# The output projection taken in thirds of its k tiles over six PSUM banks, with four expert weight pieces requested during it

## The reference

```python
def _mixer(h, ..., w_out):
    z = einsum('btd,de->bte', h, w_in) + b_in            # one input projection, 11 groups of 512
    y_r = ...    # RG-LRU group, 512 columns
    y_h = ...    # HGRN2 group, 512 columns
    y_m = sigmoid(m_o) * head_layer_norm(mlstm)          # mLSTM group, 4 heads of 128 columns
    y = concatenate([y_r, y_h, y_m], -1)                 # 1536 columns
    return einsum('bte,ed->btd', y, w_out)               # the output projection

def _layer(...):
    y = _mixer(x * (1 + sc1) + sh1, ...)
    x = layer_norm(ALPHA * x + g1 * y) * ln1_g + ln1_b
    f = _moe(x * (1 + sc2) + sh2, ...)                   # router softmax over 16 experts, best group of 4, top 2
    return layer_norm(ALPHA * x + g2 * f) * ln2_g + ln2_b

def _moe(h, ...):
    act = silu(h @ w_gate[e]) * (h @ w_up[e]) * combine  # per expert: 1024x512, 1024x512
    return act @ w_down[e]                               # 512x1024
```

## Time and profile before

| | |
|---|---|
| median of 3 runs | 750.0 us (749.65 to 751.92) |
| the profiled execution, its time | 752.23 us |
| the profiled execution, its span | 750.5 us |
| TensorE busy | 684.4 us (91%), weight loads 550.6 us |
| VectorE busy | 575.3 us (77%) |
| ScalarE busy | 433.5 us (58%) |
| GpSimd busy | 57.8 us (8%) |
| DMA | 220.06 MB, mean 293 GB/s |

### The profile page before, as it was taken

One profiled execution on the slowest core, in us unless ns is written; L12 is line 12 of the kernel. 1 busy time (PEld: TensorE's weight loads), 2 busy tenths in 40 slices (PEclk: granted clock), 3 DMA queues, 4 the chain that ended last, 5 costly groups with the idle time before them and its releaser, 6 DMA issues.

```text
span 750.5 us, 12527 instructions
## 1 busy us (share of the span) xinstructions
PE 684.4 (91%) x4818; PEld 550.6 (73%) x4818; DVE 575.3 (77%) x838; ACT 433.5 (58%) x605; POOL 57.8 (8%) x88
## 2 busy tenths in 40 slices
PE   4599989999899979999995989999999999999881
PEld 2487988898689879964454968888888888888640
DVE  2659797798993456773777878989999999999765
ACT  1647857363133445750124458888888888888721
POOL 2060000000011000132000300000000000000210
PEclk9699999999999999999996999999999999999996
DMA  9997596546758697969008999999999999999442
GB/s 334 374 244 289 203 347 230 210 155 201 279 200 280 232 396 274 334 48 385 25 0 326 411 385 396 400 398 400 400 399 400 400 399 399 400 399 400 152 144 84
DMA packets 91507, 220.06 MB, mean 293 GB/s; under 512 B 3335, under 2 KB 3631, under 8 KB 91455
## 3 DMA queue, kind: packets, MB, share of 16 engines
q1 hardware_dynamic: 85200, 200.29, 71.7%
q0 software_dynamic: 5840, 18.94, 8.4%
q10 hardware_dynamic: 415, 0.14, 0.1%
HBM read 179.99 MB, written 39.36 MB: 292 GB/s over the span
## 4 chain that ended last, share of the span: by engine, by line
PE 66%; DVE 15%; DMA 9%; ACT 4%; issue 3%; SPq 1%; POOL 1%; DVEq 0%; ACTq 0%; POOLq 0%
PE ps L1169 63%; DMA ring<-in_w_in 3%; DMA extra<-slot_rows 2%; DMA arena<-in_pos 2%; PE ps L1566 2%; DVE w_lo L1729 2%; DMA slot_rows<-arena,small 2%; DVE arena L1884 1%; DVE arena L1883 1%; DVE arena L1829 1%; PE ps L1585 1%; POOL slot_rows L749 1%; DMA ring<-in_w_gate 1%; ACT w_hi L826 1%; SPq L550 1%
## 5 line engine op out<-in xcount | busy, mean ns | idle before, releaser
L2181 DVE TENSOR_TENSOR w_lo<-arena,w_hi 128x1024 fp32r<-128x1024 f32 x96 | 114.6, 1220 | 13.8 <-ACT w_hi L1054 12.8
L2181 DVE TENSOR_TENSOR w_lo<-ring,w_hi 128x1024 fp32r<-128x1024 f32 x96 | 114.9, 1220 | 10.9 <-ACT w_hi L1054 9.8
L1054 ACT ACTIVATE w_hi<-ring 128x1024 fp32r<-128x1024 f32 x96 | 100.6, 1062 | 23.3 <-PE ps L1169 19.3
L1054 ACT ACTIVATE w_hi<-arena 128x1024 fp32r<-128x1024 f32 x96 | 100.8, 1063 | 19.6 <-PE ps L1169 13.7
L1169 PE MATMUL ps<-h_hi,w_lo 128*128 128x384 f32 x288 | 102.0, 354 | 9.4 <-DVE w_lo L1729 6.0
L1169 PE MATMUL ps<-w_hi,slot_tokens_lo 128*128 128x512 f32 x256 | 103.0, 402 | 0.8 <-DVE w_lo L2181 0.8
L1169 PE MATMUL ps<-w_hi,slot_tokens_hi 128*128 128x512 f32 x256 | 100.2, 391 | 0.0
L1169 PE MATMUL ps<-w_lo,slot_tokens_hi 128*128 128x512 f32 x256 | 99.8, 390 | 0.0
L1169 PE MATMUL ps<-h_lo,w_hi 128*128 128x384 f32 x288 | 97.5, 338 | 0.0
L1169 PE MATMUL ps<-h_hi,w_hi 128*128 128x384 f32 x288 | 97.4, 338 | 0.0
L1729 DVE TENSOR_TENSOR w_lo<-ring,w_hi 128x1024 fp32r<-128x1024 f32 x44 | 53.6, 1224 | 23.3 <-ACT w_hi L826 22.2
(11 more groups left out here) (361 smaller groups left out, 1102.7 us busy)
## 6 DMA issues: line engine op xcount, KB each, us to landing
slot_rows<-arena SPq DMA_DIRECT2D x12, 2048.0 KB, 18.3
ring<-in_w_in SPq DMA_DIRECT2D x11, 2048.0 KB, 10.0
ring<-in_w_ada SPq DMA_DIRECT2D x10, 2048.0 KB, 9.0
ring<-in_w_gate SPq DMA_DIRECT2D x8, 2048.0 KB, 18.2
ring<-in_w_up SPq DMA_DIRECT2D x8, 2048.0 KB, 18.5
ring<-in_w_down SPq DMA_DIRECT2D x8, 2048.0 KB
arena<-in_w_gate SPq DMA_DIRECT2D x8, 2048.0 KB, 18.3
arena<-in_w_down SPq DMA_DIRECT2D x8, 2048.0 KB, 14.9
```

The source lines that it names most:

```text
L1054: act.activation(w_hi[:, at_ % 4, :], raw[:, q * QUARTER:(q + 1) * QUARTER], ACT.Copy).then_inc(S["hi_ready"], 1)
L2181: tt(w_lo[:, at_ % 4, :], raw[:, q * QUARTER:(q + 1) * QUARTER], w_hi[:, at_ % 4, :].bitcast(F32), ALU.subtract).then_inc(S["lo_dve"], 1)
```

## The change

The projection is done in three sweeps. `project_all(part)` runs over all six banks with the 4 k tiles of one third of w_out: first YR, then YH. Then come the last 4 k tiles (YM) bank by bank, where the router's work is interleaved as it was. The transposes of the last mLSTM head now stand behind the first sweep, and go to bank 7 instead of bank 2. Bank waits that the order needs are added (t_taken for bank 1, cfin_sb for bank 2, h_done for bank 5).

When a sweep is over, its ring slot is free (semaphore wout_used), and SyncE requests expert weights into it: the gate of expert 2 after the first sweep, the up piece of expert 0 after the second; the down piece of expert 0 is requested at y_ready as before. The gate of expert 0 goes to a new place, `first_gate`, which is the area of `w_lo`, as soon as the last unit of the mixer's weights has been used. VectorE writes the low parts of that gate over it, quarter by quarter. `residual(1)` moves from the loop over row tiles to `last_rows`. Three one-shot semaphores become one (consts_made). The number of matmuls and the bytes moved are the same.

```diff
@@ SyncE @@
                 sp.wait_ge(S["h2_ready"], 1)
                 expert_piece(bass.ds(1, 1), 0, 1)
                 expert_piece(bass.ds(1, 1), 2, 1)
-                sp.wait_ge(S["lo_dve"], MIX_DVE + 4)
-                expert_piece(bass.ds(2, 1), 0, 0)
...
+            sp.wait_ge(S[USED[-1][0]], USED[-1][1])
+            src = a["w_gate"][0][0:1].rearrange("a (k p) n -> p (a k) n", p=P)
+            sp.dma_start(first_gate.rearrange("p (k n) -> p k n", k=KD), src).then_inc(S["gate0_in"], 16)
+            sp.wait_ge(S["wout_used"], 1)
+            expert_piece(bass.ds(2, 1), 0, 0)
+            sp.wait_ge(S["wout_used"], 2)
+            expert_piece(bass.ds(0, 1), 1, 0)
             sp.wait_ge(S["y_ready"], 2 * NT)
-            first_experts(0)
+            expert_piece(bass.ds(0, 1), 2, 0)
@@ TensorE @@
-            for m in WOUT:
-                full(m)
-            project(0, 0, range(0, 4))
+            def project_all(part):
+
+                full(WOUT[part])
+                for i in range(NT):
+                    for half in range(2):
+                        if part == 0 and (i, half) == (0, 1):
+                            pe.wait_ge(S["t_taken"], H - 1)
+                        if part == 0 and (i, half) == (1, 0):
+                            pe.wait_ge(S["cfin_sb"], 16)
+                        if part == 0 and (i, half) == (2, 1):
+                            pe.wait_ge(S["h_done"], 7)
+                        last = project(i, half, range(4 * part, 4 * part + 4))
+                last.then_inc(S["wout_used"], 1)
+
+            project_all(0)
+            normed_T(H - 1, ps[:, 7, :])
             pe.wait_ge(S["yh_full"], 1)
-            project(0, 0, range(4, 8))
-            pe.wait_ge(S["cfin_sb"], 16)
-            normed_T(H - 1, ps[:, 2, :])
-            project(0, 1, range(0, 8))
+            project_all(1)
...
             pe.wait_ge(S["ym_done"], 2)
+            full(WOUT[2])
             for i in range(NT):
-                project(i, 0, range(8 if i == 0 else 0, 12)).then_inc(S["y_ready"], 1)
+                project(i, 0, range(8, 12)).then_inc(S["y_ready"], 1)
...
-                project(i, 1, range(8 if i == 0 else 0, 12)).then_inc(S["y_ready"], 1)
+                project(i, 1, range(8, 12)).then_inc(S["y_ready"], 1)
@@ VectorE @@
                 mixed_half(i, 0)
                 router_logits(i - 1)
                 selection(i - 1)
-                residual(i - 1)
+                if i == 1:
+                    residual(0)
                 mixed_half(i, 1)
...
             def last_rows():
 
-                residual(NT - 1)
+                for i in (1, 2):
+                    residual(i)
```

More of the change, by code:

```diff
@@ L494, in build @@
                     for j, x in enumerate(("hi", "lo"))]
+        first_gate = place("first_gate", o_conv + PIECE, PIECE)
         PICK = place("picked_rows", o_conv + 2 * PIECE, 6 * D).rearrange("p (c i d) -> p c i d", c=2, i=NT)
@@ L847, in _ @@
                     act.wait_ge(S["z_ready"], Z_READY[job])
-                    act.wait_ge(S["silu_zeroed"], 1)
+                    act.wait_ge(S["consts_made"], 1)
                     act.activation(silu_w[:, 0:16].rearrange("p (k s) -> p s k", s=2), bank[:, 0:16].rearrange("p (s k) -> p s k", s=2),
@@ L1059, in landed @@
                     return ring2_full[j], 16 * pair + 16
-                return ring_full[(FIRST_EXPERT + j) % NSLOT], 16 * pair + 16 * ((FIRST_EXPERT + j) // NSLOT + 1)
+                before = (FIRST_EXPERT + j) // NSLOT
+                return ring_full[(FIRST_EXPERT + j) % NSLOT], 16 * pair + 16 * (before if j == 0 else before + 1)
             def silu(n):
@@ L1108, in expert_pass @@
                 p0 = base // 2
-                gate = expert_slot(0, 0)
+                gate = expert_slot(0, 0) if base else first_gate
                 for q in range(4):
-                    hi(base, q, gate, q, landed(0, p0, 0) if q == 0 else None)
+                    hi(base, q, gate, q, (landed(0, p0, 0) if base else (S["gate0_in"], 16)) if q == 0 else None)
                 tokens_hi(base, 0)
@@ L1309, in _ @@
                     pe.wait_ge(S[sem], value)
-                    pe.wait_ge(S["sel_ready"], 1)
+                    pe.wait_ge(S["consts_made"], 3)
                     b = job[1] // 2 % 2 if job[1] < 4 else job[1] % 2
@@ L1352, in _ @@
                     if (q, k0) == (0, 0):
-                        pe.wait_ge(S["banks_cleared"], 1)
+                        pe.wait_ge(S["consts_made"], 2)
                     w = weights(q)
@@ L1683, in _ @@
             step(dve.memset(eps, EPS))
-            step(dve.memset(silu_w, 0.0), "silu_zeroed")
+            step(dve.memset(silu_w, 0.0), "consts_made")
             step(dve.memset(zero_tile, 0.0), "zero_tile")
-            step(dve.memset(ps[:, 5:8, :], 0.0), "banks_cleared")
+            step(dve.memset(ps[:, 5:8, :], 0.0), "consts_made")
             dve.wait_ge(S["consts_in"], 16)
             step(dve.tensor_reduce(group_sel.rearrange("p (c s) -> p c s", s=2), ident.rearrange("p (c r m) -> p c m r", c=2, r=2)[:, :, 0:2, :],
-                                   AX.X, ALU.add), "sel_ready")
+                                   AX.X, ALU.add), "consts_made")
             step(dve.tensor_reduce(ident_blocks, ident.rearrange("p (j t) -> p t j", t=32), AX.X, ALU.add))
@@ L2009, in _ @@
             dve.wait_ge(S["hn_T"], H)
-            step(stt(chunk(YM, H - 1), ps[:, 2, 0:T], colsA[:, A_MLG + H - 1:A_MLG + H], chunk(MO, H - 1), ALU.mult, ALU.mult), "ym_done")
+            step(stt(chunk(YM, H - 1), ps[:, 7, 0:T], colsA[:, A_MLG + H - 1:A_MLG + H], chunk(MO, H - 1), ALU.mult, ALU.mult), "ym_done")
             def with_cols(dst, src, cols):
```

4 lines of the change are left out of this document (2 added, 2 removed).

## The result

The changed kernel takes 760.05 us (median of 4 runs, 758.53 to 761.79), the kernel before 750.38 us on the same chip (749.65 to 751.92). The ratio is 1.0126, with a 95% interval of 1.0100 to 1.0152: slower by 1.3%, a small difference, but the interval is clear of 1. The forecast was 757.7, with a range of 754 to 762. The profiled execution took 759.79 us.

A forecast was written before the change was run, and what follows sets the result against it. TensorE was taken to pace the output projection and the experts, with two stalls in the first experts. The terms +10.6 + 0.3 + 0.65 - 3.9 = +7.65 us on 750.0 gave 757.7 us, range 754 to 762.

The forecast's parts named there:

- the shift carries over: Whole kernel: the median lies 2.2 us below the profiled execution before the change, and was taken to do so after it.
- 4.1 us more: GpSimd's loads: sharing with the third weight piece makes their last 1.67 MB take 8.1 us instead of 4.1.
- rival A: LayerNorm rows: GpSimd's queue goes first, the third piece does not delay them, 375.9 decides; 755.1 us, chance 0.17.
- the equal shares: DMA: weights and GpSimd's queue each get about half of 410 GB/s when both have requests.
- The second piece: Weights requested at 345.4, just ahead of GpSimd's loads: delay of 0.3 us, bounds nothing and 5.1.
- TensorE's last four matmuls: End of projection, behind row tile 1's transposes: half clock after idling makes VectorE wait 0.3 us, bounds nothing to 2.6.
- rival B: First experts' gain fails (+3.9), or the cold clock bites in full (+2.3); 760 to 761.6 us, chance 0.17.
- The residual: residual(1) in last_rows, ahead of the low parts of expert 0's w_up: +0.65 us, bounds nothing and 2.8.
- what the reordering removes is only the wait of 4.79 us and the residual's 2.8: Up to the last evacuation: only these two savings on VectorE; the evacuation still starts 10.6 us later, at 405.9.
- The first experts' stalls: First two turns of tokens: less weight traffic behind the projection removes both stalls, -3.9 us (2.6 + 1.3).
- Rivals C and D: C: DMA truly bounds the experts, 746.3 us, chance 0.04. D: no measurable effect, late LayerNorm rows cancel early pieces, chance 0.03.

The follow-up runs named there:

- e3: Changed kernel with the last head's transposes put back behind 8 matmuls, inside the first third of the projection; 761.26 us, ratio 1.0113.
- e4b: Changed kernel with ten float32 matmuls of unused result added in TensorE's gaps around row tile 1's transposes; 755.95 us, ratio 1.0059.
- e9: Changed kernel with the last four matmuls of the projection ahead of row tile 1's transposes, not behind them; 758.09 us, ratio 1.0081.
- e5: Changed kernel with the residual of row tile 1 put back into the loop, in front of the last evacuation; 758.73 us, ratio 1.0081.
- e1: Changed kernel with all four weight pieces requested as late as in the kernel before; 762.49 us, ratio 1.0136.
- e6: Kernel before's first two banks, last head and residual; then first thirds of the other four banks; three weight pieces requested early; 745.85 us, ratio 0.9916.
- e7: Projection order of e6, with every weight piece requested as late as in the kernel before; 748.62 us, ratio 0.9981 to the kernel before.
- e4: Changed kernel with six float32 matmuls of unused result between the two halves of row tile 1's transposes; 759.89 us, ratio 1.0098.

## Why the forecast was right, and where it was not

*The mechanism held, but for what the tables wait for.* The last head's transposes came at 345.44 (forecast 345.4), the first finished bank at 370.11 (369.8), VectorE's work from the tables to the point where it waits was 403.55 - 376.16 = 27.39 us (27.4), and no steady expert became shorter: 18.11 to 18.16 us from turn to turn between 476 and 531, where the earlier trace rows give 18.14. The sum was +7.65, the trace's +7.75 counted from t0 and +7.6 by the spans. That it came out to 0.1 us is luck, as the next paragraph shows. The medians differ by 9.7 us; the 95% interval, 7.5 to 11.4 us, just reaches down to the forecast's shift. The other 2.1 us are in no stage: the profiled execution of the kernel before was 1.85 us above its median and the changed kernel's 0.26 below, so "the shift carries over" did not hold, and why stays open.

*Two terms were mis-sized and cancelled.* The step "**4.1 us more**" for the third piece put the LayerNorm rows at 378.5; they were in at 354.94 + 19.8 = 374.7, and VectorE's first row tile decided, at 376.16, as rival A has it (375.9): the forecast's path went through GpSimd's loads, the real one through the first finished bank, and e3 confirms it. So VectorE was ready for the last bank 2.2 us sooner behind t0 than forecast. Two things were wrong in the step. The larger is the time to which it was added, 360.34 - 333.29 = 27.05 us for GpSimd's queue, taken over from a trace in which that queue was slower by 4.5 us (19.2 - 14.7). The other is the equal shares, read from the means of 19 us in the earlier trace rows: the queue that was asked first went mostly first. The second piece cost some 3 us (0.3 forecast, bounds nothing and 5.1), the third at most some 2, and the two errors nearly cancel as well, 5.1 us against 4.4. Rival A's condition, GpSimd's queue first, is thus met by all but the last 0.14 MB; its 755.1 was missed through the term that follows. The rule of the Trainium skill ("DMA: Bandwidth & Descriptors", "Rules for kernel authors", issue early) gave the same 755.1; its result for this term came true, the tables did not wait for the third piece, though the transfer was not free for the last loads.

The step "**TensorE's last four matmuls**", 0.3 with bounds of nothing and 2.6, came to 3.18, above its upper bound, as the second half of rival B has it. The half clock was foreseen, its length was not: the matmuls took 5.61 us, which is in the range, but the router's took 3.60 where the forecast had the transposes and the router together at 3.4. e4b shows that the term goes when the clock stays up, e9 that it goes when the matmuls do not stand behind the transposes: it takes a wait and the half clock behind it. The clock fell within TensorE's gap of 6.17 us before 395.80 and is 0.50 from 392 to 404. Here a second page of the Trainium skill ("TensorE: Matmul & The Clock Gate", "HAM oscillation — how this bites in real kernels": in a gap the array falls to half clock and each burst starts cold) agrees with the trace.

*The residual* was priced at 0.65, and e5 shows just that in the turn, if the selection's matmuls take the same. Its other half was wrong: "what the reordering removes is only the wait of 4.79 us and the residual's 2.8". With TensorE 3.18 us late, the 2.8 bought nothing. The move costs 0.65 us, or up to 1.8 where the selection is as quick as in e5, and brings none.

*The first experts' stalls* were to give 3.9. In the changed kernel they give 2.10 + 1.49 = 3.6 net of the residual, 3.0 by e1, and 5.2 in e6 against e7, where the selection's matmuls are 0.75 us shorter than before and TensorE without the pieces idles 3.40 us and not 2.60.

*Rivals C and D* are refuted by the rows above: no expert is shorter, and the last evacuation is 11.54 us later.

## What to carry to other kernels

Freeing a buffer early by sweeping all outputs part by part finishes even the first output late: price it by the consumer that starts on the first one, here 16 us, of which 11.5 were left at the last evacuation. Take from such an order only the parts that no consumer is waiting for: the kernel with both gains (e6) is 0.8% faster than the one before, the full sweep 1.3% slower. Move work off an engine only after asking what that engine waits for next, and count the small matmuls behind a wait at half clock.

## What was not expected of the hardware

In e4 the clock fell behind gaps of 1.86, 1.02 and 1.12 us with matmuls between them: TensorE was busy for 0.14 of 2 us from 388, for all of the 4 us from 390, for 1.76 of 2 from 394 and for 0.66 of 2 from 396, and the clock was 0.50 from 400, in the middle of matmuls. With the gaps filled (5.57 of 6 us busy from 392, 5.20 of 6 from 398) it stayed at 1.00. The same code, the selection's 96 rows, begins at 0.50 in all twelve traces, and took 12.50 us where the clock came back early (e5: 0.83 in the stretch of 2 us that begins 2.5 us behind the first row) and 13.79 where it came late (e4: 0.62 in the one that begins 4.4 us behind it). And the same load on the same queue took 14.7 us from issue to landing with nothing beside it (e1), 19.8 with two weight pieces beside it (changed kernel), and 19.2 with the modulation rows issued 8 us ahead and not 22 (before).
